# Nine pairs of weight tiles by seven half-size products, and a denser order of steps, in a one-core trunk layer

## The reference

```
xn = RMSNorm(x);  [q|k|v|o|i|f|u|g] = xn @ w_in            # 65 tiles of 128 output rows
h  = mLSTM(q, k, v, i, f)          # 4 heads x 256, chunkwise: 8 chunks of 128 and the sample, per head
ya = (headnorm(h) * sigmoid(o)) @ w_proj_a
c  = silu(LayerNorm(causal_dwconv31(u[:1024] * sigmoid(u[1024:]))));  yb = c @ w_proj_b
x  = x + RMSNorm((sigmoid(gA) * ya + sigmoid(gB) * yb) @ w_out)
up = causal_dwconv3(RMSNorm(x) @ w_up);  x = x + RMSNorm((gelu(up[:2816]) * up[2816:]) @ w_down)
```

## Time and profile before

| | us |
|---|---|
| median of 3 runs (lowest, highest) | 1961.7 (1960.69, 1962.05) |
| the profiled execution | 1961.44 |
| its span, first to last instruction | 1959.7 |
| TensorE busy | 1939.0 (99%) |
| VectorE busy | 1268.7 (65%) |
| ScalarE busy | 775.1 (40%) |

### The profile page before, as it was taken

One profiled execution on the slowest core, in us unless ns is written; L12 is line 12 of the kernel. 1 busy time (PEld: TensorE's weight loads), 2 busy tenths in 40 slices (PEclk: granted clock), 3 DMA queues, 4 the chain that ended last, 5 costly groups with the idle time before them and its releaser, 6 DMA issues.

```text
span 1959.7 us, 30693 instructions
## 1 busy us (share of the span) xinstructions
PE 1939.0 (99%) x12783; PEld 1916.0 (98%) x12783; DVE 1268.7 (65%) x1655; ACT 775.1 (40%) x1423; POOL 23.4 (1%) x59
## 2 busy tenths in 40 slices
PE   9999999999999999999999999999999999999997
PEld 8999999999999999999999999999999999999997
DVE  6896777776777754443445548977777767636363
ACT  5422222322323234463222335644544544635242
POOL 0000000000000000000000000000000000000000
PEclk9999999999999999999999999999999999999999
DMA  3221122212111334655531304112212212656554
GB/s 133 66 73 49 51 61 73 59 51 90 56 56 48 120 110 149 192 177 210 193 134 43 138 27 150 67 67 88 78 67 88 78 67 96 199 197 202 203 177 157
DMA packets 90138, 212.61 MB, mean 108 GB/s; under 512 B 15372, under 2 KB 50572, under 8 KB 90000
## 3 DMA queue, kind: packets, MB, share of 16 engines
q1 hardware_dynamic: 90000, 210.64, 32.2%
HBM read 160.24 MB, written 50.37 MB: 107 GB/s over the span
## 4 chain that ended last, share of the span: by engine, by line
PE 90%; DVE 6%; DMA 2%; ACT 1%; issue 1%; SPq 0%; POOL 0%; DVEq 0%; ACTq 0%; POOLq 0%
PE ps L855 17%; PE ps L856 17%; PE ps L857 17%; PE ps L1122 7%; PE ps L1123 7%; PE ps L1124 7%; PE ps L1140 4%; PE ps L1141 4%; PE ps L1142 4%; PE ps L926 2%; PE ps L923 1%; DVE cacc L1875 1%; DMA scr_xc<-cs 1%; PE ps L906 1%; PE ps L924 1%
## 5 line engine op out<-in xcount | busy, mean ns | idle before, releaser
L855 PE MATMUL ps<-rx,fhi 128*128 128x364 f32 (+2 forms) x1752 | 585.8, 334 | 0.4 <-DVE flo L1698 0.4
L857 PE MATMUL ps<-rx,flo 128*128 128x364 f32 (+2 forms) x1752 | 571.8, 326 | 0.0
L856 PE MATMUL ps<-rx,fhi 128*128 128x364 f32 (+2 forms) x1752 | 571.6, 326 | 0.0
L1875 DVE SCALAR_TENSOR_TENSOR cacc<-glub,pars,cacc 128x1118 f32<-128x1118 f32 x240 | 331.6, 1381 | 5.6
L855 PEld LDWEIGHTS ps<-rx,fhi 128*128 128x128 f32 x1752 | 329.5, 188 | 2.6 <-issue 1.1
L856 PEld LDWEIGHTS ps<-rx,fhi 128*128 128x128 f32 x1752 | 329.7, 188 | 1.5
L857 PEld LDWEIGHTS ps<-rx,flo 128*128 128x128 f32 x1752 | 329.3, 188 | 0.0
L1140 PE MATMUL ps<-ghi,dhi 128*128 128x384 f32 (+1 forms) x528 | 173.6, 329 | 2.5 <-DVE glo L2189 2.2
L1142 PE MATMUL ps<-ghi,dlo 128*128 128x384 f32 (+1 forms) x528 | 172.6, 327 | 0.0
L1141 PE MATMUL ps<-glo,dhi 128*128 128x384 f32 (+1 forms) x528 | 172.6, 327 | 0.0
L2182 DVE TENSOR_TENSOR dlo<-draw,dhi 128x1408 fp32r<-128x1408 f32 x48 | 77.7, 1625 | 119.0 <-ACT dhi L1583 119.0
(11 more groups left out here) (281 smaller groups left out, 3992.0 us busy)
## 6 DMA issues: line engine op xcount, KB each, us to landing
fraw<-wts SPq DMA_DIRECT2D x84, 512.0 KB, 3.7
draw<-wdn SPq DMA_DIRECT2D x48, 704.0 KB, 4.2
uraw<-wts SPq DMA_DIRECT2D x44, 512.0 KB, 4.4
scr_g<-cva SPq DMA_DIRECT2D x22, 512.0 KB, 2.6
graw<-scr_g SPq DMA_DIRECT2D x43, 192.0 KB, 4.1
fx<-x SPq DMA_DIRECT2D x8, 544.0 KB, 8.4
scr_ga<-spl SPq DMA_DIRECT2D x8, 544.0 KB, 5.0
scr_gb<-spl SPq DMA_DIRECT2D x8, 544.0 KB, 4.2
```

The costliest lines, as they stand in the source:

```text
L855: pe.matmul(b, hi[:, w], src[:, his[k], cols], start=(k == 0), stop=False)
L856: pe.matmul(b, hi[:, w], src[:, los[k], cols], start=False, stop=False)
L857: mm = pe.matmul(b, lo[:, w], src[:, his[k], cols], start=False, stop=(k == KB - 1))
L1875: op = dve.scalar_tensor_tensor(a[:, :], g[:, j:j + AW], pars[:, at:at + 1], a[:, :], ALU.mult, ALU.add)
```

## The change

In the front, nine pairs of tiles are done by the seven half-size products: (ga, gb) for blocks 0 to 6 and (ua, ub) for blocks 2 and 3, in the order `PAIRS_B`, all in one stretch between slots 17 and 18 (before the gate tile). The list of whole tiles falls from 65 to 47.

- TensorE: `pairs` does 14 groups of 12 matmuls a pair, in the order `ORDER_B` (the first pair `ORDER_0`). A group's name is (product, half): half 0 has 304 columns, half 1 240. Products 1 and 6, 7 and 4 add up in one bank, and ScalarE copies the piece out between them.
- SP: four loads of 256 KB a pair (`pair_weights`), each issued once a group of the pair in work is done: weights 1 of pair i+1 after (7,1) of pair i-1, weights 2 after (1,1) of pair i, weights 7 after (5,1), weights 4 after (6,1). They lie in ten slots of `araw`. The seven operands of the next pair are made of these four on VectorE (4 sums) and rounded on ScalarE (7 copies), their 7 remainders taken on VectorE.
- VectorE: also adds products 5, 2 and 3 to the pieces (`piece_onto`, 6 a pair), and does 6 conv taps a pair.
- x: sums of its blocks (`x_sums`), their rounded parts and remainders are made once. They take the place of half of `rx`, which is saved to `scr_b12` (2 x 1.1 MB) and reloaded during the last pair.
- Steps: at slots 18+22+3i and 18+52+3i for heads 0 and 1, 18+82+2i and 18+100+2i for heads 2 and 3 (before: every fourth). Conv blocks 2 to 7 take 14 slots each (before 18). `PASS1` and `PASS2` are placed anew, `PASS2` with one or two slots between blocks. Scores lie in another bank and wait for `hn` of the step before, where they waited for `zs`; ScalarE's `rows_out` comes ahead of its `values`.
- Every remainder of a whole tile is VectorE's (`N_BY_DVE = N_IN`), as it was before; a path by accumulating transfers is in the text and is given no tile.

```diff
-    return (pair(0) + pair(1) + [("gate", 0)] + head(0, "kvq") + pair(2) + head(1, "k") + [("v", 2)] + pair(3)
-            + [("v", 3)] + head(1, "q") + one("ga", 0, 1) + pair(4) + head(2, "kv") + pair(5) + head(2, "q")
-            + one("ga", 1, 3) + pair(6) + head(3, "kv") + pair(7) + head(3, "q") + one("ga", 3, KB)
-            + one("gb", 0, KB) + one("o", 0, KB))
+    return (pair(0) + pair(1) + one("o", 0, 1)
+            + [("gate", 0)] + head(0, "kvq") + pair(4) + head(1, "kv") + pair(5) + head(1, "q") + pair(6)
+            + head(2, "k") + pair(7) + head(2, "vq") + head(3, "kvq") + [("ga", 7), ("gb", 7)] + one("o", 1, KB))
...
+N_A = 5
+S_B = 3 * XN + 3 * (N_A - 3)
+PAIRS_B = [("g", 0), ("g", 1), ("g", 2), ("g", 3), ("g", 4), ("u", 2), ("g", 5), ("g", 6), ("u", 3)]
...
+ORDER_0 = ((1, 0), (1, 1), (2, 0), (2, 1), (5, 0), (5, 1), (6, 0), (6, 1), (7, 0), (7, 1), (4, 0), (4, 1), (3, 0), (3, 1))
+ORDER_B = ((1, 0), (1, 1), (5, 0), (5, 1), (6, 0), (6, 1), (2, 0), (7, 0), (7, 1), (2, 1), (4, 0), (4, 1), (3, 0), (3, 1))
...
+STEP_AT = [S_B + at for at in [22 + 3 * i for i in range(9)] + [52 + 3 * i for i in range(9)]
+           + [82 + 2 * i for i in range(9)] + [100 + 2 * i for i in range(9)]]
...
+            def pairs():
+                for i, (kind, k) in enumerate(PAIRS_B):
...
+                        sp.wait_ge(grp_done, b_at(i, 5, 1))
+                        pair_weights(i + 1, 7)
+                        sp.wait_ge(grp_done, b_at(i, 6, 1))
+                        pair_weights(i + 1, 4)
...
+                    if TAPS_B * i >= CW and TAPS_B * (i - 1) < CW:
+                        store_conv(0)
...
+            def a_hi(i, prod):
+                s = aslot(i, prod)
+                act.wait_ge(a_in[i % 2], 64 * (i // 2 + 1))
...
+                    piece(i, 6, 0)
+                    if i + 1 < NB:
+                        a_hi(i + 1, 1)
+                    piece(i, 6, 1)
...
+                    if i + 1 < NB:
+                        pair_sums(i + 1)
+                        a_rest(i + 1, 1)
+                    piece_onto(i, 5, 0), piece_onto(i, 5, 1)
+                    if i + 1 < NB:
+                        pair_sums(i + 1, True)
+                    piece_onto(i, 2, 0), piece_onto(i, 2, 1)
+                    if i + 1 < NB:
+                        a_rest(i + 1, 5), a_rest(i + 1, 6), a_rest(i + 1, 2)
+                    some_taps(t + TAPS_B // 2, t + TAPS_B)
+                    if i + 1 < NB:
+                        a_rest(i + 1, 7), a_rest(i + 1, 4), a_rest(i + 1, 3)
+                piece_onto(NB - 1, 3, 0), piece_onto(NB - 1, 3, 1)
+                rest(N_A), rest(N_A + 1)
```

More of the change, by code:

```diff
@@ L215 @@
 DH_W = FB // 2 * P
-W_DOWN = (16 * FB, 16 * (N_RING // 3))
+W_IN = [16 * sum(1 for i in range(n % 3, n + 1, 3) if not N_BY_DVE <= i < N_IN) for n in range(N_RING)]
+W_DOWN = [[16 * FB + AB_IN[p] for p in range(2)], [max(W_IN[n] for n in range(p, N_RING, 3)) for p in range(2)]]
 N_DN = N_STR + (FB - N_PLAIN) * len(PAIR)
@@ L446, in build @@
         w_lo = sem("w_lo")
+        w_cast = sem("w_cast")
+        w_acc = [sem(f"w_acc{s}") for s in range(2)]
         grp_done = sem("grp_done")
@@ L604, in _ @@
                         sp.dma_start(decs[:, h, :], scr_dec[h].partition_broadcast(P)).then_inc(decs_in, 16)
[L606 to L612, removed]
+                if s == S_B + 5:
+                    store_conv(1)
+                for j, at in CONV_AT.items():
+                    if s == at + CONV_SLOTS + 1:
+                        store_conv(j)
                 if s and is_last(s - 1) and SLOTS[s - 1][0] in TANH_OUT:
@@ new lines, in piece, with pairs @@
+            def piece(i, prod, u):
+                b = bank(2 * (i % 2) + u, 0, XP[2 * u][1])
+                act.wait_ge(grp_done, b_at(i, prod, u))
+                dst = v0[i % 2] if prod in (1, 6) else v1
+                p = 2 * u + (prod in (6, 7))
+                act.activation(dst[:, pcut(p)], b, ACT.Copy).then_inc({1: p1_set, 6: u2_set, 7: u3_set, 4: c21_set}[prod], 1)
+            def pairs():
+                part_whole(0, 1), part_whole(1, 1)
+                for i in range(NB):
+                    if V0_STORES[i % 2][i]:
+                        act.wait_ge(spl_out[i % 2], 16 * V0_STORES[i % 2][i])
+                    if i >= 2 and PAIRS_B[i - 2][0] == "u":
+                        act.wait_ge(tanh_set, 1 + 3 * sum(kind == "u" for kind, _ in PAIRS_B[:i - 1]))
+                    piece(i, 1, 0), piece(i, 1, 1)
+                    if i == 0:
+                        part_whole(0, 2), part_whole(1, 2)
+                    else:
+                        first_of(i - 1)
+                    piece(i, 6, 0)
+                    if i + 1 < NB:
+                        a_hi(i + 1, 1)
+                    piece(i, 6, 1)
+                    if i and PAIRS_B[i - 1][0] == "g":
+                        act.wait_ge(v1_out, 16 * G_BEFORE[i])
+                    elif i:
+                        act.wait_ge(glu_set, 2 * PAIRS_B[i - 1][1] + 2)
+                    piece(i, 7, 0)
+                    piece(i, 7, 1)
+                    if i + 1 < NB:
+                        a_hi(i + 1, 5), a_hi(i + 1, 6), a_hi(i + 1, 2), a_hi(i + 1, 7), a_hi(i + 1, 4)
+                    piece(i, 4, 0), piece(i, 4, 1)
+                    if i + 1 < NB:
+                        a_hi(i + 1, 3)
+                    else:
+                        whole(N_A)
+                    second_of(i)
+                whole(N_A + 1)
```

582 lines of the change are left out of this document (466 added, 116 removed).

## The result

| | before | changed |
|---|---|---|
| median of the runs | 1961.7 us | 1970.77 us (5 runs, 1969.89 to 1971.55) |
| ratio to before | | 1.0046, 95% interval 1.0036 to 1.0057 |
| profiled execution | 1961.44 | 1971.55 |
| its span | 1959.7 | 1969.7 |
| TensorE busy | 1939.0 | 1926.0 |

The changed kernel is 9.1 us slower. The forecast was 1960, 1.7 less than before. The measured time lies just inside the upper edge of the wide range (1947 to 1971), outside the likeliest case's own (1955 to 1966), and slower where the sum had a small gain. That the wide range holds it is luck: its upper part stood for rivals B and C, and neither happened (no wait for a reload, the 256 KB loads at 2.6 us).

The account below looks back on a forecast made before the run. TensorE was taken as the bound, busy 1939.0 of 1959.7 us. Terms -25.7 + 2.7 + 4.9 + 13.5 + 3.0 + 0.1 = -1.5 gave 1960 us, range 1947 to 1971, likeliest case 1955 to 1966.

Parts of the forecast that it names:

- likeliest case: The prediction's own sum of gains and gaps holds, 1960 us, range 1955 to 1966, chance 0.38.
- rival B: Steps every second slot beside the layernorm's reloads: late reloads hold up VectorE, then TensorE; 1970 to 1976 us, chance 0.14.
- C: Pair loads land at 3.9 us because they share queues with large stores: +8 us, 1968, chance 0.14.
- Term 1: TensorE's work in the nine pairs: half-size products take 21.09 us a pair instead of 23.95, -25.7 us.
- Terms 2 to 4: Gaps in the pairs: late fourth load +2.7 us, VectorE's order +4.9, start, end and single-pair waits +13.5.
- term 3: Steady pairs: VectorE's chain before product 5 is 0.8 us late in six pairs, +4.9 us.
- Term 5: Gate chain: VectorE's remainder after scans and exponents is later, behind an added tap and block 3's `gated`: +3.0 us.
- Term 6: Steps closer together, every three or two slots: VectorE still fits, net +0.1 us, bounds -2 and +12.
- the conv layernorm beside it 0.8: In the 2-slot steps for heads 2 and 3: the conv layernorm costs 0.8 us beside a step.

Follow-up runs that it names:

- holds: Kernel before, TensorE made to wait once near the front's end for 5, 8 or 11 VectorE products: 1965.34, 1967.38 and 1969.22 us.
- early store: Changed kernel with the tail of conv block 0 stored at the end of the sixth pair, not the seventh: 1965.83 us.
- light gate stretch: Changed kernel with block 3's gated instructions seven slots later and block 2's conv taps spread towards later slots: 1964.4 us.
- first version with all edits: Changed kernel with five edits: earlier store, taps ahead of sums, lighter gate stretch, second pass's last block earlier, product 6's piece first: 1948.55 us.
- last block's edit alone: Changed kernel with the last block of the conv layer norm's second pass one slot earlier (122, was 123): 1969.29 us.
- short hold: Kernel before, TensorE made to wait once, before the front's last slot but one, for 5 VectorE products: 1965.34 us.

## Why the prediction was wrong, point by point

**Term 1** (-25.7) is right: the same window as in the up stage, once the waits are gone. (The spacing rule that it sets beside its own stands in the section "Wait — 56ns, not 53.3ns?" of that page of the Trainium skill; the sum did not use it.)

**Terms 2 to 4** (21.1 us of waits in the block of pairs) are right in place and near in sum. The block ran from 79.34 to 289.90, 210.6 us for a counted 211. The 256 KB loads landed in 2.6 us (median of the 36), as taken. In a steady pair the period was 22.5 (130.37 to 152.86) for a counted 22.35; the two waits in it are recorded as 0.23 and 0.59, and each shows as 0.1 to 0.3 more from start to start. The chain of term 3 is right row by row; its 0.27 for passing the word between the engines had no row behind it. Single sizes: the conv tail's store landed in 2.2 us and not 3.2, which is 1.0 of what the seventh pair's gap (3.1 for 4.3) and the eighth's (1.4 for 3.3) are short of; the rest of the eighth's is not accounted for. Of the 210.6 us 1.7 are the half-rate stretch, which was in no term; without it the waits come to 19.1, counted from start to start (13.6 in the view of waits). So the near hit of the block, 210.6 for 211, is in part luck: 2.0 less of waits and 1.7 of clock.

**Term 5** (+3.0) is right in its mechanism and small by 1.1: a wait of 4.5 us where 3.7 was counted. (The two things that it names, a tap of 1.4 and `gated` of 1.3, come to 2.7.) The start of the program gave 0.8 us more, where the sums of x, counted as hidden, made one remainder late at 55.

**Term 6** (+0.1) failed. Of its parts the 3-slot steps are right (no wait up to 700), and the 2-slot steps gave 1.5 us in two waits for `hn` (1.2 behind three taps and a sum, where 1.1 was counted) for the 1.8 that went; rival B, the reloads, did not happen. The part that failed is "the conv layernorm beside it 0.8": the second pass now ends in the last slot of the front, and TensorE waits 4.2 us for its last remainder at the start of the next stage, 3.6 more than the 0.6 that stood there before. The slots were there to be counted: the pass's three parts stand in slots 123, 124 and 125 after the pairs, and 125 is the last. The prediction has what the pass does to the steps beside it, and nothing of what waits for its end.

**The sum's rule failed.** All its terms price a gap at its length, with the clock full. Three gaps passed 3 us, and the clock fell at each, for 3.4, 6.8 and 6.8 us. Part of that lies in the gaps themselves; in work it took 1.7, 2.7 and 2.4 us. That is 6.8 us in no term, of which 1.7 are in the block's 210.6. The holds show the effect alone. The Trainium skill has the fall and the two levels ("TensorE: Matmul & The Clock Gate", section "What's actually happening"); the prediction read the clock as a constant. The trace of before has no gap long enough to show what one costs, but it has the fall itself: TensorE's last matmul ends at 1949.0, and the clock is at half from 1950.4 on.

```profile
1950.00:1955.00 5.00, 0.00 (x0) 0.00 (x0) 4.88 (x4) 0.02 (x1) 0.00 (x0) 0.54 0.18 65
```

Put together, in spans: -25.7 + 20.8 (the block's waits with its 1.7 of clock) + 4.1 (gate chain) + 0.8 (start) + 0.1 (steps) + 3.6 (end of the second pass) + 5.1 (clock, behind the gate chain and the second pass) + 0.8 (a bank emptied late near 898) = +9.6, measured +10.0. The largest single part that was in no term is the clock (6.8), then the end of the second pass (3.6).

The edits bear this out: the early store gave back 4.9 for waits that the view has as 2.6 shorter in all (5.8 to 3.8 and 6.6 to 6.0), the light gate stretch 6.4 for a wait of 4.5. The rest is clock, in the first case partly that of the two later gaps.

## What to carry to other kernels

Don't price a gap of the tensor engine by its length alone. In these traces all nineteen gaps from 2.7 us on went with 3.4 or 6.8 us at half clock, which by their part in work cost some 1.5 to 3 us more than the gap. Of the dozen gaps from 1.8 to 2.4 us one did, so no length in that range is safe by these runs. One gap of 4 us then costs 5.5 to 7 us (an estimate from these). When a stage is made shorter, list what ends in its last slots and who waits for it at once, not only what it runs beside. Where a helper engine has time over in each period, put its movable work at the point where it waits for a transfer, not between the pieces that the bounding engine wants.

## What was not expected of the hardware

- By the trace's record of the clock, it fell 2.1 to 4.4 us after TensorE had stopped, in half of the twenty cases while the engine still stood idle and in the others when it was at work again for up to 1.3 us, and stayed at half for 3.4 or 6.8 us. The same gap of 4.5 us had 6.8 us in one kernel and 3.4 in the next; what decides it was not found.
- A gap of 2.7 us in the first version with all edits went with 3.4 us at half clock (0.83 over the 10 us from 104), and so did one of 1.8 with the last block's edit alone; one of 2.4 in the short hold did not.
- Two stores of 15 KB landed in 2.2 us in the changed kernel, issued behind a load of 256 KB, and in 3.2 in the kernel before, where two loads and a store of 544 KB were issued in the same 8 us.
